# Expert layer: three-pass fp32r products, a fixed tile for each group and three more by index

## The chip, the core and the metric

The kernel runs on one core of a Trainium2 chip. The metric is device time in microseconds. Engines: TensorE (PE, its weight loads PEld), VectorE (DVE), ScalarE (ACT), GpSimd (POOL) and SyncE (SP, which here only issues DMAs).

## The reference

A block with two attention branches and a layer of hierarchical experts, then a second block. What the change touches is the expert layer on 512 rows `h` of width 1024:

```
g_sel  = argmax(h @ w_router_group + b)          # one of 8 groups for each row
top2   = top 2 of the 4 experts of that group    # by h @ w_router_expert
for e in 32 experts:
    hid = silu(h @ w_gate[e]) * (h @ w_up[e])    # 1024 -> 256
    out += (hid @ w_down[e]) * combine[:, e]     # 256 -> 1024, weight 0 if not chosen
```

`h` is the RMS norm of the residual `X` times the weights `norm_ffn_g`. All is float32.

## The kernel before

Rows are sorted by group, so that a tile of 128 rows needs only the four experts of its group. Block one (L949 to L1057) makes the norm (`Norm`, L277: squares on ScalarE, scaling of rows on VectorE into `XN`, transposes on TensorE, copies to `HT` with the norm weights as a scale for each partition), the router logits, the routing arithmetic on VectorE (some 60 small instructions), a slot number for each row (`SL_`) and for each unit the row numbers of its weights (`IX`). A group takes as many tiles of 128 as its count needs; eleven tiles (`NT`) are enough for any input. GpSimd then scatters the rows of `XN` with their four expert weights to `HS` in HBM. During this block SP loads three weight tiles for the block after the experts (L952).

Block two (L1089 to L1208) runs over 44 units n = 4j + x, tile j, expert x:

- GpSimd gathers the unit's weights by index: 2 MB into one of three `UP` (gate and up side by side, 8 x 512 columns), 1 MB into one of four `DN`.
- SP loads the tile's rows `HR` and stores the finished tile `OT` to `OS`.
- TensorE, step by step: the up product of unit n (8 f32 matmuls of 512 columns into `bank[n % 2]`), two transposes of the hidden rows of unit n-1, the down product of unit n-2 (4 f32 matmuls, summed over the tile's four units in two banks), and in steps 2 and 3 of a tile four transposes each of the next tile (`pe_tile`, L1072).
- ScalarE: silu of unit n (L1168), copy of the transposed hidden rows of n-1 (L1174), half of the output copy (L1181).
- VectorE: silu times up times the row's expert weight (L1194), half of the output copy (L1202), and at the end of a step the copy of the transposed tile times the norm weights into `HX` (`dve_tile`, L1082).

After the last unit GpSimd gathers the rows of `OS` back by slot and VectorE adds them to `X` (L1208). Every engine works through its list in order; waits are on counting semaphores, so an instruction also holds all that stands behind it on its engine. Each `nc.Block()` ends with all engines meeting. `sb2` gives a buffer a second name on the same memory for its fp32r content.

In other stages the kernel already multiplies split operands: ScalarE copies an operand rounded to fp32r (high part), VectorE subtracts that from the operand (low part), and TensorE makes three passes, low x high, high x low, high x high (L843 to L845, L2275 to L2277).

Of the kernel before, what the change touches and what calls it, by code (L numbers as in the profile page):

```python
# [83 lines left out]
def lay(i):  # L84
# [54 lines left out]
    for name, key in (("qd", "g_q_dil_2"), ("kd", "g_k_dil_2"), ("qm", "g_q_mem_2"), ("km", "g_k_mem_2")):  # L139
# [6 lines left out]
            "un": i["peer_u_2"][0], "vn": i["peer_v_2"][0], "grow": np.ascontiguousarray(np.broadcast_to(i["g_ffn_2"][0], (128, 1024))), "gains": g, "consts": consts, "bd": bd}, sizes  # L146
# [36 lines left out]
def program(nc, d, out, sizes):  # L183
    ctx = ExitStack()
    with ctx:
# [741 lines left out]
        NT = 11  # L927
        NU = 4 * NT
        HS, OS = d["hs"], d["os"]
        with ExitStack() as c0:  # L930
            XN = sb("XN", [128, 4, 1028], c0)
            SL_ = sb("slot", [128, 4], c0, I32)
            IX = sb("IX", [128, NU], c0, I32)
            scattered = sem("scattered", True)
            with ExitStack() as c1:
                norm = Norm(c1, "ffn", 1, 1, HT, "ffn", rows=XN)
                LG, GO, EX = sb("LG", [128, 4, 40], c1), sb("GO", [128, 4, 8], c1), sb("EX", [128, 4, 8], c1)
# [7 lines left out]
                GT, GI, IF = sb("GT", [128, NT, 8], c1), sb("GI", [128, NT], c1), sb("IF", [128, NT, 4], c1)  # L945
# [3 lines left out]
                with nc.Block() as block:  # L949
                    @block.sync  # L950
                    def _(e):
                        load_weights(e, 24)  # L952
# [18 lines left out]
                    @block.scalar  # L971
                    def _(e):
                        norm.act_sums(e)
                        norm.act_root(e)
                        norm.act_keep(e)
                        e.wait_ge(*e_off(1))
                        e.activation(EX, EX, ACT.Exp).then_inc(*e_exp.up(1))
                        e.wait_ge(*e_off2(1))
                        e.activation(s1[:, 3, :], s1[:, 2, :], ACT.Exp).then_inc(*e_exp2.up(1))

                    @block.vector
                    def _(e):
# [3 lines left out]
                        norm.dve_rows(e)  # L986
                        norm.dve_keep(e)
# [45 lines left out]
                        then(e.tensor_scalar(TL, RK[:, 4, :], 0.0, None, ALU.is_gt))  # L1033
                        for j in range(1, 4):
# [4 lines left out]
                        then(e.tensor_scalar(T9, T8, 128.0, None, ALU.mult))  # L1039
                        then(e.tensor_tensor(RK[:, 0:4, :], RK[:, 0:4, :], T9.unsqueeze(1).to_broadcast([128, 4, 8]), ALU.add))  # L1040
# [3 lines left out]

                        then(e.tensor_tensor(GT, EN.unsqueeze(1).to_broadcast([128, NT, 8]),
                                             col(cc("iota")[:, 0:NT]).to_broadcast([128, NT, 8]), ALU.is_le))
                        then(e.tensor_reduce(GI, GT, AX.X, ALU.add))
                        then(e.tensor_scalar(GI, GI, 7.0, 512.0, ALU.min, ALU.mult))
                        then(e.tensor_tensor(IF, cc("rows").unsqueeze(1).to_broadcast([128, NT, 4]), col(GI).to_broadcast([128, NT, 4]), ALU.add))
# [9 lines left out]
            UP = [sb(f"UP{n}", [128, 4096], c0) for n in range(2)] + [HT.rearrange("p k n -> p (k n)")]  # L1059
            DN = [sb(f"DN{n}", [128, 2048], c0) for n in range(4)]  # L1060
            HR = [sb(f"HR{n}", [128, 1028], c0) for n in range(2)]
            HX = [sb(f"HX{n}", [128, 8, 128], c0) for n in range(2)]
            SLU, HN = ([sb(f"{x}{n}", [128, 256], c0) for n in range(2)] for x in ("SLU", "HN"))
            HH = [sb(f"HH{n}", [128, 256], c0) for n in range(3)]
            OT = [sb(f"OT{n}", [128, 1024], c0) for n in range(2)]
            (m_hturn, m_hx, m_up, m_silu, m_hn, m_turn, m_hh, m_down, m_outA, m_outV, m_add) = sems(
                "m_hturn m_hx m_up m_silu m_hn m_turn m_hh m_down m_outA m_outV m_add")
            up_in, dn_in = [sem(f"up_in{n}", True) for n in range(3)], [sem(f"dn_in{n}", True) for n in range(4)]
            hr_in, os_done = [sem(f"hr_in{n}") for n in range(2)], [sem(f"os_done{n}") for n in range(2)]
            yg_in = sems("yg_in0 yg_in1 yg_in2 yg_in3", True)  # L1070

            def pe_tile(e, j, part):  # L1072

                if part == 0:
                    e.wait_ge(*hr_in[j % 2](16 * (j // 2) + 16))
                if 2 * j + part:
                    e.wait_ge(*m_hx(2 * j + part))
                for q in range(4):
                    i = e.transpose(bank[3][:, span(q)], HR[j % 2][:, span(4 * part + q)], ident)
                i.then_inc(*m_hturn.up(1))  # L1080

            def dve_tile(e, j, part):  # L1082
                e.wait_ge(*m_hturn(2 * j + part + 1))
                if j >= 2:
                    e.wait_ge(*m_up(4 * (j - 2) + 4))
                g4 = gg("ffn")[:, span(part, 4)].unsqueeze(2).to_broadcast([128, 4, 128])
                e.tensor_tensor(HX[j % 2][:, span(part, 4), :], bank[3].rearrange("p (a b) -> p a b", a=4), g4, ALU.mult).then_inc(*m_hx.up(1))  # L1087

            with nc.Block() as block:  # L1089
                @block.gpsimd  # L1090
                def _(e):
                    for n in range(NU):
                        off = bass.IndirectOffsetOnAxis(ap=IX[:, n:n + 1], axis=0)
                        if n >= 3:
                            e.wait_ge(*m_up(n - 2))
                        e.indirect_dma_start(UP[n % 3], None, d["wup"][:, :], off).then_inc(*up_in[n % 3].up(16))
                        if n >= 4:
                            e.wait_ge(*m_down(n - 3))
                        off = bass.IndirectOffsetOnAxis(ap=IX[:, n:n + 1], axis=0)
                        e.indirect_dma_start(DN[n % 4], None, d["wdn"][:, :], off).then_inc(*dn_in[n % 4].up(16))  # L1100
                    for n in range(2):
                        e.wait_ge(*os_done[n](16 * ((NT + 1 - n) // 2)))
# [5 lines left out]
                def _(e):  # L1108
                    e.wait_ge(*scattered(64))
                    for j in range(NT + 2):  # L1110
                        if j < NT:
                            if j >= 2:
                                e.wait_ge(*m_hn(4 * (j - 2) + 4))
                            e.dma_start(HR[j % 2], HS[span(j), :]).then_inc(*hr_in[j % 2].up(16))
                        if j >= 2:
                            e.wait_ge(*m_outA(j - 1))
                            e.wait_ge(*m_outV(j - 1))
                            e.dma_start(OS[span(j - 2), :], OT[j % 2]).then_inc(*os_done[j % 2].up(16))

                @block.tensor  # L1120
                def _(e):
                    pe_tile(e, 0, 0)
                    pe_tile(e, 0, 1)
                    for step in range(NU + 2):
                        n = step
                        if n < NU:
                            j = n // 4
                            e.wait_ge(*m_hx(2 * j + 2))
                            e.wait_ge(*up_in[n % 3](16 * (n // 3) + 16))
                            if n >= 2:  # L1130
                                e.wait_ge(*m_hn(n - 1))
                            for k in range(8):
                                i = e.matmul(bank[n % 2], HX[j % 2][:, k, :], UP[n % 3][:, span(k, 512)], start=k == 0, stop=k == 7)  # L1133
                            i.then_inc(*m_up.up(1))
                        n = step - 1
                        if 0 <= n < NU:
                            e.wait_ge(*m_hn(n + 1))
                            if n:
                                e.wait_ge(*m_hh(n))
# [4 lines left out]
                        if 0 <= n < NU:  # L1144
                            j, x = divmod(n, 4)
                            e.wait_ge(*m_hh(n + 1))
                            e.wait_ge(*dn_in[n % 4](16 * (n // 4) + 16))
                            if x == 0 and j >= 2:
                                e.wait_ge(*m_outA(j - 1))
                                e.wait_ge(*m_outV(j - 1))  # L1150
                            for half_ in range(2):
                                for q in range(2):
                                    i = e.matmul(bank[4 + 2 * (j % 2) + half_], HH[n % 3][:, span(q)], DN[n % 4][:, span(2 * q + half_, 512)],  # L1153
                                                 start=x == 0 and q == 0, stop=x == 3 and q == 1, skip_group_check=True)
                            i.then_inc(*m_down.up(1))
                        j, x = divmod(step, 4)
                        if x >= 2 and j + 1 < NT:
                            pe_tile(e, j + 1, x - 2)

                @block.scalar  # L1160
                def _(e):
                    for step in range(NU + 2):
# [7 lines left out]
                        if 0 <= n < NU:  # L1170
# [3 lines left out]
                            e.activation(HH[n % 3], bank[2][:, 0:256], ACT.Copy).then_inc(*m_hh.up(1))  # L1174
                        n = step - 2
                        if 0 <= n < NU and n % 4 == 3:
                            j = n // 4
                            e.wait_ge(*m_down(n + 1))
                            if j >= 2:
                                e.wait_ge(*os_done[j % 2](16 * (j // 2)))  # L1180
                            e.activation(OT[j % 2][:, 512:1024], bank[5 + 2 * (j % 2)], ACT.Copy).then_inc(*m_outA.up(1))  # L1181

                @block.vector
                def _(e):
                    dve_tile(e, 0, 0)
# [1167 lines left out]
```

## Time and profile before

| | us |
|---|---|
| runs | 3452.49, 3452.99, 3468.13 |
| median | 3452.99 |
| profiled execution, first to last instruction | 3467.7 |
| of it the expert block, first row load to the next block's first instruction | 672.4 to 1183.6 |

The page gives for the whole span TensorE 88% busy, VectorE 50%, ScalarE 31%, GpSimd 14%, and a mean granted clock of 0.93. These are means over some fifteen stages; the expert stage is read by itself. A busy TensorE is not TensorE at its peak, and the duration of a matmul record is longer than the distance to the next one, since matmuls overlap; rates are taken from starts. An f32 matmul leaves two records, an fp32r pass one.

### The profile page before, as it was taken

The page shows a single profiled execution, that of the slowest core. Times are in us where ns is not written, and L with a number is a line of the kernel's source. Part 1 is how long each engine was busy: PE and PEld are TensorE (multiplying, and loading weights), DVE is VectorE, ACT ScalarE, POOL GpSimd, SP SyncE. Part 2 cuts the span into 40 slices and gives each one's busy share as a digit, 9 for nine tenths or more (in the row PEclk, how much of TensorE's full clock was granted, in tenths as well). Part 3 has the DMA queues.
Part 4 walks back from the last instruction along what each step waited for, and adds up shares of the span by engine and source line. Part 5 has one row for each costly group of instructions (what it writes and reads, how often), then busy time and mean ns, then how long its engine had stood idle before and what let it go on. Part 6 is the DMA issues. An engine that isn't in the chain of part 4 may idle for free. (4 is left out here: it accounts for less than half of the span.)

```text
span 3467.7 us, 33649 instructions
## 1 busy us (share of the span) xinstructions
PE 3066.9 (88%) x12681; PEld 2229.5 (64%) x12681; DVE 1723.3 (50%) x3505; ACT 1076.1 (31%) x1596; POOL 488.8 (14%) x357
## 2 busy tenths in 40 slices
PE   7887999699999598778979879698898986999998
PEld 3445666444444244564746568698898986888887
DVE  2255422200000205543442328787879797788886
ACT  2133421100000126674421222234434443333332
POOL 0000000111111000000000000003314143344442
PEclk9995999699999798889779989899999998999999
DMA  3110061488888210021002211357859688999996
GB/s 142 44 50 25 1 145 64 194 329 309 313 315 309 85 49 37 25 97 44 1 26 102 83 55 61 123 193 246 324 178 336 233 305 292 342 369 374 368 374 238
DMA packets 159776, 624.04 MB, mean 180 GB/s; under 512 B 12161, under 2 KB 84481, under 8 KB 128257
## 3 DMA queue, kind: packets, MB, share of 16 engines
q1 hardware_dynamic: 90496, 319.87, 26.1%
q0 software_dynamic: 50688, 276.85, 21.1%
q10 hardware_dynamic: 18432, 25.17, 2.0%
q8 instruction: 102, 1.67, 0.2%
q14 instruction: 58, 0.47, 0.0%
HBM read 555.76 MB, written 66.09 MB: 179 GB/s over the span
## 5 line engine op out<-in xcount | busy, mean ns | idle before, releaser
L1841 POOL DMA_INDIRECT RG<-in_un,EI x128 | 181.6, 1419 | 1400.0 <-DVE EI L2060 1105.3
L2275 PE MATMUL bank<-VH,GL 128*128 128x512 f32 x768 | 300.2, 391 | 29.9 <-DVE VR0r L2264 29.9
L2277 PE MATMUL bank<-VH,GH 128*128 128x512 f32 x768 | 299.7, 390 | 0.0
L1841 POOL DMA_INDIRECT RG<-in_vn,EI x128 | 216.5, 1691 | 446.7 <-DVE X L1855 429.9
L1133 PE MATMUL bank<-UP,HX 128*128 128x512 f32 x480 | 213.0, 597 | 9.4 <-DVE HX L1087 5.5
L1194 DVE SCALAR_TENSOR_TENSOR HN<-SLU,HR,bank 128x256 f32<-128x256 f32 x44 | 21.1, 481 | 344.2 <-ACT SLU L1168 344.2
L2275 PEld LDWEIGHTS bank<-VH,GL 128*128 128x128 f32 x768 | 144.8, 189 | 60.7 <-issue 30.4
L1855 DVE SCALAR_TENSOR_TENSOR X<-RG,DG,X 128x1024 f32<-128x1024 f32 x128 | 164.1, 1282 | 28.2 <-DMA RG<-in_vn,EI 24.1
L1825 PE MATMUL bank<-HTl,UH1r 128*128 128x384 f32 x512 | 174.5, 341 | 0.0
L1826 PE MATMUL bank<-HTh,UH1r 128*128 128x384 f32 x512 | 174.2, 340 | 0.0
L1825 PE MATMUL bank<-HTl,UH0r 128*128 128x384 f32 x512 | 173.3, 338 | 0.0
L1826 PE MATMUL bank<-HTh,UH0r 128*128 128x384 f32 x512 | 173.0, 338 | 0.0
L618 PE MATMUL bank<-W,HT 128*128 128x512 f32 (+2 forms) x384 | 155.1, 558 | 19.1 <-ACT SU L685 14.4
L1445 PE MATMUL bank<-W,HT 128*128 128x384 f32 (+2 forms) x448 | 163.2, 523 | 8.3 <-ACT SV L1491 8.3
L1133 PEld LDWEIGHTS bank<-UP,HX 128*128 128x128 f32 x480 | 90.6, 191 | 119.9 <-issue 112.7
L1852 DVE CUSTOM_DVE_ANT_0 RG<-RG,HR 128x1024 f32<-128x1024 f32 x128 | 155.7, 1220 | 20.7 <-DMA RG<-in_un,EI 20.7
L2277 PEld LDWEIGHTS bank<-VH,GH 128*128 128x128 f32 x768 | 144.9, 189 | 30.3
L2259 ACT ACTIVATE VH<-VR 128x2048 fp32r<-128x2048 f32 x64 | 119.6, 1910 | 130.8 <-DMA VR<-in_vn 122.8
L1153 PE MATMUL bank<-DN,HH 128*128 128x512 f32 x352 | 158.2, 592 | 0.0
L2181 ACT ACTIVATE GA<-bank 128x384 f32<-128x384 f32 x128 | 62.8, 491 | 296.3 <-PE bank L1826 296.2
L2276 PE MATMUL bank<-VR0r,GH 128*128 128x512 f32 x384 | 150.5, 392 | 0.0
L2103 PE MATMUL bank<-OB,OA 128*128 128x128 f32 x768 | 107.5, 287 | 48.2 <-DVE OB L2095 48.2
(518 smaller groups left out, 6569.3 us busy)
## 6 DMA issues: line engine op xcount, KB each, us to landing
UR<-in_u SPq DMA_DIRECT2D x64, 1024.0 KB, 5.5
VR<-in_vn SPq DMA_DIRECT2D x32, 2048.0 KB, 9.2
W<-in_weights SPq DMA_DIRECT2D x20, 1536.0 KB, 7.3
W<-in_weights SPq DMA_DIRECT2D x14, 2048.0 KB, 8.2
aspill<-GA ACTq DMA_DIRECT2D x128, 192.0 KB, 2.0
wspill<-VR SPq DMA_DIRECT2D x12, 2048.0 KB, 9.2
WW<-wspill SPq DMA_DIRECT2D x32, 768.0 KB, 13.9
AV<-aspill SPq DMA_DIRECT2D x32, 768.0 KB, 16.0
```

The lines of the kernel that those rows point to most:

```text
L618: i = e.matmul(bank[n % 2][:, 0:nw], lhs(k, tb), w[:, span(k, nw)], start=k == 0, stop=k == KK[t] - 1)
L1133: i = e.matmul(bank[n % 2], HX[j % 2][:, k, :], UP[n % 3][:, span(k, 512)], start=k == 0, stop=k == 7)
L1153: i = e.matmul(bank[4 + 2 * (j % 2) + half_], HH[n % 3][:, span(q)], DN[n % 4][:, span(2 * q + half_, 512)], start=x == 0 and q == 0, stop ...
L1445: i = e.matmul(bank[4 + u % 2][:, 0:w], lhs(k), weight(t)[:, span(k, w)], start=k == 0, stop=k == 7)
L1825: e.matmul(bk, r(hi[:, k, :]), r(HL_[:, k, 0:NT3]), start=False, stop=False)
L1826: i = e.matmul(bk, r(hi[:, k, :]), r(HH_[:, k, 0:NT3]), start=False, stop=k == 7)
L1841: e.indirect_dma_start(RG[q % RR], None, d["un" if what == "u" else "vn"][:, :], off).then_inc(*row_in[q % RR].up(16))
L1852: e.tensor_tensor_reduce(RG[q % RR], RG[q % RR], HR3, 1.0, 0.0, ALU.mult, ALU.add, DT[:, s:s + 1]).then_inc(*r_used.up(1))
L1855: e.scalar_tensor_tensor(X[:, 3, :], RG[q % RR], DG[:, s:s + 1], X[:, 3, :], ALU.mult, ALU.add).then_inc(*r_used.up(1))
L2275: e.matmul(bk, r(gl[:, a, t]), r(vh[:, a, :]), start=g == 0 and a == 0, stop=False)
L2276: e.matmul(bk, r(gh[:, a, t]), r(vl[:, a, :]), start=False, stop=False)
L2277: i = e.matmul(bk, r(gh[:, a, t]), r(vh[:, a, :]), start=False, stop=g == 31 and a == 3)
```

## The change

- Tiles: each of the eight groups has one fixed tile, whose weights SP loads by plain DMAs (`load_up`, `load_dn`) without an index. Rows beyond 128 of a group go to three more tiles (`NO`), whose weights are gathered by index; an index beyond the table moves nothing. `SEQ` mixes the 32 fixed and 12 indexed units, one indexed after every 2.5. 44 units remain.
- Products: both are made in three fp32r passes. ScalarE rounds and VectorE subtracts the unit's weights (4096 and 2048 columns), the tile's transposed rows and the transposed hidden rows. High parts of weights lie in the memory of the three `W` buffers.
- Norm weights: `FR` holds them as rows; VectorE applies them with the row scale in one operation, so neither the copies to `HT` nor those of the tile need them.
- Routing block: SP loads `FR`, up weights of units 0 and 1 and down weights of units 0 to 2. The three weight tiles for the next block are loaded after the last output store.
- Output: one `OT` in place of two, copied by ScalarE alone; one pair of banks for fixed tiles and one for indexed.

```diff
-        NT = 11
-        NU = 4 * NT
+        NT, NO = 8, 3
+        NU = 4 * (NT + NO)
+        SEQ = []
+        for k in range(4 * NT):
+            SEQ.append((k // 4, k % 4))
+            for o in range(4 * NO):
+                if int(2.5 * (o + 1)) == k:
+                    SEQ.append((NT + o // 4, o % 4))
...
+        BUILDS = sorted(((FIRST_AT[t] - 2 + part, t, part) for t in range(NT + NO) for part in range(2)))
...
                     def _(e):
-                        load_weights(e, 24)
+                        e.dma_start(FR, d["frow"]).then_inc(*fr_in.up(16))
+                        load_weights(e, 21)
+                        load_up(e, 0)
+                        load_dn(e, 0)
+                        load_up(e, 1)
+                        load_dn(e, 1)
+                        load_dn(e, 2)
...
-                        norm.dve_rows(e)
-                        norm.dve_keep(e)
+                        norm.dve_scale(e)
+                        e.wait_ge(*fr_in(16))
+                        for b in range(4):
+                            e.scalar_tensor_tensor(XN[:, b, 0:1024], X[:, b, :], norm.o[:, b:b + 1], FR, ALU.mult, ALU.mult).then_inc(*n_rows.up(1))
...
+            def act_build(e, t, part):
+                b = BUILT[t, part]
+                e.wait_ge(*m_hturn(b + 1))
+                if before(t) >= 0:
+                    e.wait_ge(*m_up(LAST_AT[before(t)] + 1))
+                e.activation(r(HXh[place(t) - 1][:, span(part, 4), :]), bank[3].rearrange("p (a b) -> p a b", a=4), ACT.Copy).then_inc(*m_hxh.up(1))
+
+            def dve_build(e, t, part):
+                b = BUILT[t, part]
+                e.wait_ge(*m_hxh(b + 1))
+                s = span(part, 4)
+                e.tensor_tensor(r(HXl[place(t) - 1][:, s, :]), bank[3].rearrange("p (a b) -> p a b", a=4), HXh[place(t) - 1][:, s, :], ALU.subtract).then_inc(*m_hxl.up(1))
...
+            def act_up(e, n):
+                e.wait_ge(*(up_in if NORMAL(n) else up_over)[n % 3](nth(n)))
+                if n >= 2:
+                    e.wait_ge(*m_up(n - 1))
+                for half_ in range(2):
+                    c = span(half_, 2048)
+                    e.activation(r(UH[n % 2][:, c]), UP[n % 3][0][:, c], ACT.Copy).then_inc(*m_uph.up(1))
...
                 @block.sync
                 def _(e):
                     e.wait_ge(*scattered(64))
+                    for t in (0, 1, NT):
+                        load_rows(e, t)
+                    load_up(e, 2)
+                    for step in range(NU + 2):
+                        n = step + 3
+                        if n < NU and NORMAL(n):
+                            e.wait_ge(*m_up(n - 2))
+                            load_up(e, n)
...
+                        n = step + 1
+                        if 3 <= n < NU and NORMAL(n):
+                            e.wait_ge(*m_down(n - 2))
+                            load_dn(e, n)
+                        n = step - 2
+                        if 0 <= n < NU and SEQ[n][1] == 3:
+                            t = SEQ[n][0]
+                            e.wait_ge(*m_out(2 * ENDED.index(t) + 2))
+                            e.dma_start(OS[span(t), :], OT).then_inc(*os_done.up(16))
+                    load_weights(e, 24)
...
                 @block.tensor
...
+                            e.wait_ge(*m_hxl(BUILT[t, 1] + 1))
                             if n >= 2:
                                 e.wait_ge(*m_hn(n - 1))
                             for k in range(8):
-                                i = e.matmul(bank[n % 2], HX[j % 2][:, k, :], UP[n % 3][:, span(k, 512)], start=k == 0, stop=k == 7)
+                                if k % 4 == 0:
+                                    e.wait_ge(*m_upl(2 * n + k // 4 + 1))
+                                c = span(k, 512)
+                                e.matmul(bank[n % 2], r(xl[:, k, :]), r(wh[:, c]), start=k == 0, stop=False)
+                                e.matmul(bank[n % 2], r(xh[:, k, :]), r(wl[:, c]), start=False, stop=False)
+                                i = e.matmul(bank[n % 2], r(xh[:, k, :]), r(wh[:, c]), start=False, stop=k == 7)
...
+                        for t, part in builds(step):
+                            pe_build(e, t, part)
...
                 @block.scalar
...
                             if n >= 3:
                                 e.wait_ge(*m_down(n - 2))
-                            e.activation(HH[n % 3], bank[2][:, 0:256], ACT.Copy).then_inc(*m_hh.up(1))
+                            e.activation(r(HHh[n % 3]), bank[2][:, 0:256], ACT.Copy).then_inc(*m_hhh.up(1))
+                            act_down(e, n)
+                        n = step + 2
+                        if n < NU:
+                            act_up(e, n)
...
+                            if ENDED.index(t):
+                                e.wait_ge(*os_done(16 * ENDED.index(t)))
+                            for half_ in range(2):
+                                e.activation(OT[:, span(half_, 512)], bank[(4 if t < NT else 6) + half_], ACT.Copy).then_inc(*m_out.up(1))
+                        for t, part in builds(step):
+                            act_build(e, t, part)
...
                 @block.vector
...
+                        n = step - 1
+                        if 0 <= n < NU:
+                            e.wait_ge(*m_hhh(n + 1))
+                            e.tensor_tensor(r(HHl[n % 3]), bank[2][:, 0:256], HHh[n % 3], ALU.subtract).then_inc(*m_hhl.up(1))
+                            dve_down(e, n)
+                        n = step + 2
+                        if n < NU:
+                            dve_up(e, n)
+                        for t, part in builds(step):
+                            dve_build(e, t, part)
```

`dve_up`, `act_down` and `dve_down` follow the form of `act_up`: the subtraction waits for the rounding (of the same half), the low part is written over the loaded weights. Down weights are split in one piece of 2048 columns. `FIRST_AT[t]` is the place of a tile's first unit in `SEQ`.

## Rows read from the trace of the kernel before

**Rows 1.** Busy time by stretch: length, PE, PEld, DVE, ACT, POOL, PEclk, DMA share, GB/s

```profile
1000.00:1100.00 100.00, 98.43 (x254) 44.77 (x253) 9.16 (x16) 7.71 (x21) 16.86 (x18) 1.00 0.81 309
```

**Rows 2.** Timeline of TensorE: start, us, engine, line, operation, idle before and releaser

```profile
895.91 0.60 PE L1079 MATMUL bank<-C,HR 128*128 128x128 f32 x4
...
897.29 7.13 PE L1133 MATMUL bank<-HT,HX 128*128 128x512 f32 x16 [0.78 <-DVE HX L1087]
...
904.26 0.38 PE L1141 MATMUL bank<-C,HN 128*128 128x128 f32 x2
904.48 3.60 PE L1153 MATMUL bank<-DN,HH 128*128 128x512 f32 x8
907.92 7.03 PE L1133 MATMUL bank<-UP,HX 128*128 128x512 f32 x16
...
914.78 0.38 PE L1141 MATMUL bank<-C,HN 128*128 128x128 f32 x2
```

**Rows 3.** Timeline of TensorE in two stages with three fp32r passes

```profile
599.87 0.40 PE L843 MATMUL bank<-WH,YL 128*128 128x512 f32 x1
...
604.77 0.40 PE L843 MATMUL bank<-WH,YL 128*128 128x512 f32 x1
...
3300.15 0.39 PE L2275 MATMUL bank<-VH,GL 128*128 128x512 f32 x1
...
3302.19 0.39 PE L2275 MATMUL bank<-VH,GL 128*128 128x512 f32 x1
```

**Rows 4.** Timeline of ScalarE and VectorE, then two lines' durations (min/median/max)

```profile
904.46 0.38 ACT L1168 ACTIVATE SLU<-bank 128x256 f32<-128x256 f32 x1 [11.35 <-PE bank L1133]
...
2977.09 3.73 ACT L2259 ACTIVATE VH<-VR 128x2048 fp32r<-128x2048 f32 x2 [4.72 <-DMA VR<-in_vn]
...
629.58 2.74 DVE L302 TENSOR_SCALAR XN<-X,rtffn 128x1024 f32<-128x1024 f32 x4
...
1190.44 4.87 DVE L1290 SCALAR_TENSOR_TENSOR X<-X,rtfin,G 128x1024 f32<-128x1024 f32 x4
...
L2264 DVE TENSOR_TENSOR VR0r<-VR,VH x32: 2281/2286/2294, 2930.0 to 3429.9; 128x2048 fp32r<-128x2048 f32 x32
...
L1087 DVE TENSOR_TENSOR HX<-bank,G x22: 691/692/693, 676.9 to 1116.6; 128x512 f32<-128x512 f32 x22
```

**Rows 5.** Timeline of TensorE: restart and first pass at full rate, twice

```profile
580.21 0.80 PE L843 MATMUL bank<-WH,YL 128*128 128x512 f32 x1 [2.77 <-DVE YL L897]
...
583.30 0.39 PE L844 MATMUL bank<-W0r,YH 128*128 128x512 f32 x1
...
1993.80 0.80 PE L843 MATMUL bank<-WH,YL 128*128 128x512 f32 x1 [12.04 <-DVE YL L897]
...
2000.09 0.39 PE L843 MATMUL bank<-WH,YL 128*128 128x512 f32 x1
```

**Rows 6.** DMA issues: count, KB each, median us from issue to landing

```profile
W<-in_weights SPq DMA_DIRECT2D x14, 2048.0 KB, 8.2
...
UP<-in_wup,IX POOLq DMA_INDIRECT x30, 10.4
...
XN<-os,slot POOLq DMA_INDIRECT x4, 5.3
...
RG<-in_un,EI POOLq DMA_INDIRECT x128, 8.5
```

**Rows 7.** Timeline of SP's queue and TensorE around the expert stage

```profile
672.42 0.80 SPq L1114 DMA_DIRECT2D HR<-hs  x2
...
682.65 15.44 PE L1133 MATMUL bank<-UP,HX 128*128 128x512 f32 x32 [3.91 <-DMA UP<-in_wup,IX]
...
1155.88 0.38 PE L1141 MATMUL bank<-C,HN 128*128 128x128 f32 x2
```

**Rows 8.** Timeline of GpSimd and ScalarE at the stage's end

```profile
1170.44 0.94 POOL L1105 DMA_INDIRECT XN<-os,slot  x1 [30.58 <-DMA os<-OT]
...
1183.62 1.06 ACT L289 ACTIVATE xnfin<-X 128x1024 f32<-128x1024 f32 x1 [16.20 <-PEq L1089]
```

More of the change, by code:

```diff
@@ L974, in _ @@
                         norm.act_root(e)
-                        norm.act_keep(e)
+                        for k in range(0, 8, 2):
+                            e.wait_ge(*n_turn(8 + k + 1))
+                            e.activation(HT[:, k, :], bank[k], ACT.Copy).then_inc(*n_keptA.up(1))
                         e.wait_ge(*e_off(1))
@@ L1032, in _ @@
                         then(e.tensor_copy(RK, bank[1][:, 0:40].rearrange("p (b g) -> p b g", b=5)))
-                        then(e.tensor_scalar(TL, RK[:, 4, :], 0.0, None, ALU.is_gt))
-                        for j in range(1, 4):
+                        then(e.tensor_scalar(TL, RK[:, 4, :], 128.0, None, ALU.is_gt))
+                        for j in range(2, 4):
                             then(e.tensor_scalar(T8, RK[:, 4, :], 128.0 * j, None, ALU.is_gt))
@@ L1064, in program @@
[L1064 to L1069, printed above, removed]
@@ L1070, in program @@
-            yg_in = sems("yg_in0 yg_in1 yg_in2 yg_in3", True)
-            def pe_tile(e, j, part):
+            UH = [W2[0][1], W2[1][1]]
+            DH = [W2[2][1][:, span(n, 2048)] for n in range(2)]
+            OT = XN[:, 0, 0:1024]
+            place = lambda t: 1 + (t % 2 if t < NT else 2)
+            HR = lambda t: XN[:, place(t), :]
+            HXh, HXl = ([sb(f"{x}{n}", [128, 8, 128], c0) for n in range(3)] for x in ("HXh", "HXl"))
+            SLU, HN = ([sb(f"{x}{n}", [128, 256], c0) for n in range(2)] for x in ("SLU", "HN"))
@@ new lines, in program @@
+            HHh, HHl = ([sb(f"{x}{n}", [128, 256], c0) for n in range(3)] for x in ("HHh", "HHl"))
+            (m_hturn, m_hxh, m_hxl, m_uph, m_upl, m_dnh, m_dnl, m_up, m_silu, m_hn, m_turn, m_hhh, m_hhl, m_down, m_out, m_add) = sems(
+                "m_hturn m_hxh m_hxl m_uph m_upl m_dnh m_dnl m_up m_silu m_hn m_turn m_hhh m_hhl m_down m_out m_add")
+            hr_in, os_done = [sem(f"hr_in{n}") for n in range(3)], sem("os_done")
+            yg_in = sems("yg_in0 yg_in1 yg_in2 yg_in3", True)
@@ L1089, in program, with dve_down @@
+            def dve_down(e, n):
+                e.wait_ge(*m_dnh(n + 1))
+                e.tensor_tensor(r(DN[n % 3][1]), DN[n % 3][0], DH[n % 2], ALU.subtract).then_inc(*m_dnl.up(1))
             with nc.Block() as block:
@@ L1091, in _ @@
                 def _(e):
[L1092 to L1102, printed above, removed]
+                    for step in range(-3, NU):
+                        n = step + 3
+                        if 2 <= n < NU and not NORMAL(n):
+                            x = 4 * (SEQ[n][0] - NT) + SEQ[n][1]
+                            if n >= 3:
+                                e.wait_ge(*m_up(n - 2))
+                            e.indirect_dma_start(UP[n % 3][0], None, d["wup"][:, :], bass.IndirectOffsetOnAxis(ap=IX[:, x:x + 1], axis=0),
+                                                 bounds_check=4095, oob_is_err=False).then_inc(*up_over[n % 3].up(16))
+                        n = step + 1
+                        if 3 <= n < NU and not NORMAL(n):
+                            x = 4 * (SEQ[n][0] - NT) + SEQ[n][1]
+                            e.wait_ge(*m_down(n - 2))
+                            e.indirect_dma_start(DN[n % 3][0], None, d["wdn"][:, :], bass.IndirectOffsetOnAxis(ap=IX[:, x:x + 1], axis=0),
+                                                 bounds_check=4095, oob_is_err=False).then_inc(*dn_over[n % 3].up(16))
+                    e.wait_ge(*os_done(16 * (NT + NO)))
                     for tb in range(4):
```

167 lines of the change are left out of this document (99 added, 68 removed).

## Prediction

> **What bounds the kernel now.** The changed stage is the expert stage: 44 units (11 tiles of 128 token rows, 4 experts each). [...] The timeline of TensorE says what it does in a unit: two transposes (0.22 us), 8 records of the down product (3.44 us), 16 records of the up product (6.86 us), together 10.52 us from one unit to the next, with nothing idle [rows 2]. A full f32 matmul is two records of 0.43 us, 0.86 us. Each tile also takes two groups of four transposes (0.44 us each at 0.11 us, the spacing of the unit's two), and after the second TensorE waits for VectorE's copy: 1.38 us in all, of which 0.94 is this wait [rows 2]. Remember that wait: the second group sits directly ahead of the tile's first up product, and the change lengthens what lies between.
>
> **What the change removes and adds on TensorE.** Each product of a split f32 pair is three fp32r passes. The trace has such triples in two other stages: seven triples in 4.90 us (0.233 us a pass) and three in 2.04 us (0.227) [rows 3]. I take 0.230 and keep both ends. Three passes are 0.69 us against 0.86. A unit becomes 24 passes up (5.52), 12 down (2.76) and the transposes (0.22): 8.50 us against 10.52. If that were all, 44 units would save some 85 us. The number of units stays 44: the three tiles by index are computed whether filled or not. [...]
>
> **What it adds on ScalarE and VectorE.** For each unit ScalarE now rounds 4096 + 2048 columns of weights to fp32r and VectorE subtracts them. The price is that of the last stage's split: a ScalarE copy of 2048 columns, two in 3.73 us, so 1.82 us apiece with a 1.91 us end-to-end; a VectorE subtraction 2.29 us, and 2.20 from start to start, since consecutive VectorE instructions overlap by about 0.08 (four of 1.28 us take 4.87) [rows 4]. ScalarE: 0.38 + 0.38 + 3 x 1.82, plus copies for tiles, about 6.5 to 8 us a unit. VectorE: 0.48 + 0.4 + 3 x 2.20, about 7.5, plus 0.69 in steps with a tile build. Both are under 8.50, so neither sets the steady pace. That is not the end of it, since the order within the queues matters.
>
> **The new wait.** Call U the moment when TensorE has issued the up product of unit s. ScalarE then does silu, the copy of the hidden rows and the down rounding (ends U + 2.7: 0.2 from the transposes at 904.26 to silu at 904.46 [rows 2, 4], 0.28 for each of the two small ones, 1.91), then the two up roundings for unit s+2, ending U + 4.5 and U + 6.3. VectorE waits for the down rounding, and does its three subtractions from U + 2.7: ends at U + 5.0, 7.2, 9.4. Only then, last in its step, stands the subtraction for the tile being built (0.69 us, as the same shape in [rows 4]), ending at U + 10.0. The second half of a tile is built in the step just ahead of the tile's first unit, so the next up product waits for that: it can start at U + 10.15, whereas TensorE has finished transposes, down product and build at U + 0.22 + 2.76 + 0.44 = U + 3.4. TensorE idles 6.7 us. In steps with no second half the up product needs only what VectorE did a step earlier (slack over 4 us), and the down product likewise. The order of units puts second halves in steps 2, 4, 10, 15, 16, 21, 26, 30, 32 and 38: ten stalls. The ScalarE copy of the tile (about 0.6) and the output copies come before it, but end by U + 7.8 and are hidden under VectorE; if VectorE were idle they would cost at most 2 us.
>
> **The clock after each stall.** [...] Half rate for 4.5 us loses 4.5 x (1 - 0.230/0.427) = 2.1 us; bounds 1.4 and 2.9. So a step with a stall is 10.15 + 5.52 + 2.1 = 17.8 us, against 8.50 without and 8.94 with a first half.
>
> **Loads.** The 32 fixed units are loaded by SP with plain DMAs, 2 MB up and 1 MB down. SP issues the up load of unit n when the up product of n-3 is done, and ScalarE wants it 10.8 us later or more (11.5 ahead of a stall). A plain 2 MB load lands in 8.2 us [rows 6], so it is hidden, by 2.6 us; late loads would show in the stalls one for one. On SP, the row loads and the output stores stand behind waits that end by U + 7.8, before the next load is due. The reference's router, worked out on the given inputs, sends 52 to 75 tokens to each of the 8 groups, so no group exceeds 128 and the three indexed tiles are empty: their 12 units have indexes beyond the table. No row shows what a gather costs whose rows all are out of bounds; it lies between nothing and a full load (10.4 us as now [rows 6]), and both ends are hidden under the 10.8 us. What it does bring is less traffic, which nothing waits for.
>
> **Before the loop.** The norm weights on the rows: four three-operand row operations cost 4.87 us where four scalings cost 2.74 [rows 4], and the transposes follow them: +2.1. The scale-free copies out of PSUM save under 0.1 and I take zero. The slot arithmetic has one small VectorE instruction more, 0.2. So all engines enter the expert block 2.3 us later, at 674.7 instead of 672.4 [rows 7]. The 7 MB loaded early have landed by then, so the wait for the first weights (3.91 us [rows 7]) goes, but what is late next is VectorE: it splits unit 0 first (to 681.1), then the first half of tile 0 (681.7), TensorE turns the second half at half clock (1.1, twice the 0.60 of [rows 2] less overlap), ScalarE copies 0.6, VectorE subtracts 0.7: first up product at 684.3, against 682.65. If ScalarE's table load stands first instead of ahead of the first silu, 1.3 more.
>
> **The sum.** U(0) = 684.3 + 5.5 + 2.1 = 691.9. U(1) = 697.4. U(2) = 703.1. In step 2 VectorE is still 3.5 us behind from the start, so the third up product starts at 715.6, and U(3) = 723.2. From there 40 steps: 9 stalls x 17.8, 0.4 for the double build in step 15, 31 x 8.50, 8 first halves x 0.44: 427.6. U(43) = 1150.8, against 1155.88 now [rows 7]. The 2.0 us a unit bring some 85 us, ten stalls take 67, the clock takes 23 with the one at the start, and the old stage's own waits (10 x 0.94) are gone: what is left is 5.
>
> **The end.** Now the final gather starts 14.6 us after U(43) [rows 7, 8]. After: the down split of unit 42 holds its product till U + 5.1, that of unit 43 till U + 8.0, and its output copy must wait for the store of the indexed tile from the same single buffer (about 2.8 us from store to release): gather at U + 16.2, +1.6. The gather of the outputs then competes with three 2 MB weight loads that formerly ran during routing and now are issued right behind the last store. Gathers of this size land in 5.3 us there now, and in 8.5 us in the stage with saturated DMA [rows 6]: I take +3.6 for the last of four, bounds 0 and 7. The weights themselves are needed 26 us after the next block's start and land in time. Sum: 1150.8 + 16.2 + 13.2 (gather to next block [rows 8]) + 3.6 = 1183.8, against 1183.62: **no change**. The profiled execution took 3467.7 us; the runs were 3452.49, 3452.99 and 3468.13, so the profile resembles the highest. No difference against the median gives 3453. Terms of the range: pass interval +-5 (1464 passes on the path by 0.0033), clock -7 to +10, gather +-3.5, start +1.3, length of stalls +-3: roughly 3440 to 3465 for this case by itself.
>
> **Rivals.**
> Clock kept (faster): were the clock not lowered by the ten 6.7 us stalls, 21 us would come back: 3432. Against: every row with more than 2.7 us idle shows it lowered.
> [...]
> No stall (faster): if VectorE reached the tile's subtraction before U + 3.4, stalls and clock losses vanish: about -88 us, 3365. It needs VectorE to reorder or to be three times as quick; its subtraction times vary under 1%.
> [...]
> Late weights (slower): if plain loads land later than 11.5 us after issue, every stall grows by the excess. The output stores, row loads and down loads share the queue; the same size lands in 8.2 us at the median but the gathers now in 10.4. At 13.8 us: 10 x 2.3, 3476.
> That the change doesn't do what it says: the three passes and the queue order stand in the code, so there is little room; included in the above.
>
> **How the numbers follow.** Forecast 0.68, clock kept 0.07, pace of the clock 0.03, no stall 0.04, half clock long 0.08, late weights 0.10. Within 0.5% (17 us, about what a measurement of this kernel can tell from no change) lies the forecast but for 0.04 on either side. Faster: 0.14 + 0.04 = 0.18. Slower: 0.18 + 0.04 = 0.22. Same: 0.60. The range goes from just below the kept clock (3430) to just past the late weights (3478).
>
> **What would show it.** Right: a spacing of 8.5 us between up products, ten gaps of 6 to 7 us on TensorE each released by VectorE's tile subtraction, passes of 0.43 us behind each, a mean clock in the stage near 0.9, U(43) near 1151. Wrong: gaps released by a DMA or by ScalarE's rounding (late weights), passes at full rate behind gaps, a steady spacing above 9 us (then VectorE or ScalarE sets the pace).

## The result

| | median, us | ratio of the fast runs to those of before | 95% interval |
|---|---|---|---|
| before | 3452.99 | 1 | |
| after | 3471.26 | 1.0035 | 1.002 to 1.005 |

The change made the kernel slower by 0.35% (0.2 to 0.5%), some 12 us. The forecast was no change (3453, within 17 us). The profiled execution of after has a span of 3491.4 us against 3467.7, but 16.1 of these 23.7 us arise ahead of the changed stage, in an attention stage that the change doesn't touch (last section). So the profiles are compared by stage, each from its own start: from the first instruction of the routing block to the first of the block behind the experts it was 560.9 us (622.76 to 1183.62) and is 569.0 (638.87 to 1207.87), 8.1 us more.

The page of after, shares of the span:

```profile
PE 3021.3 (87%) x13209; PEld 2351.6 (67%) x13209; DVE 2022.8 (58%) x3672; ACT 1329.7 (38%) x1761; POOL 435.7 (12%) x293
...
UP<-in_wup SPq DMA_DIRECT2D x22, 2048.0 KB, 8.0
DN<-in_wdn SPq DMA_DIRECT2D x32, 1024.0 KB, 7.3
```

VectorE and ScalarE have 300 and 254 us more work, TensorE 46 less, and yet the span isn't shorter. The busy time by stretch in the middle of the expert stage (length, PE, PEld, DVE, ACT, POOL, granted clock, DMA share, GB/s) answers to [rows 1]:

```profile
755.00:1100.00 345.00, 299.49 (x1262) 239.38 (x1263) 239.49 (x170) 203.03 (x187) 25.45 (x18) 0.91 0.59 224
```

TensorE was 98% busy at clock 1.00 and set the pace of the stage; now it is 87% busy at 0.91. It waits, and it is slowed. Where, the timeline around tile 9 shows. TensorE (answers to [rows 2]):

```profile
877.34 0.38 PE L1256 MATMUL bank<-C,HN 128*128 128x128 f32 x2
877.47 0.48 PE L1271 MATMUL bank<-W2r,HHl 128*128 128x512 f32 x1
...
880.34 0.60 PE L1138 MATMUL bank<-C,XN 128*128 128x128 f32 x4
887.38 0.79 PE L1246 MATMUL bank<-W1r,HXl 128*128 128x512 f32 x1 [6.44 <-DVE HXl L1152]
...
888.82 0.63 PE L1246 MATMUL bank<-W1r,HXl 128*128 128x512 f32 x1
890.10 0.63 PE L1246 MATMUL bank<-W1r,HXl 128*128 128x512 f32 x1
...
893.73 0.39 PE L1246 MATMUL bank<-W1r,HXl 128*128 128x512 f32 x1
894.43 0.39 PE L1246 MATMUL bank<-W1r,HXl 128*128 128x512 f32 x1
895.13 0.39 PE L1246 MATMUL bank<-W1r,HXl 128*128 128x512 f32 x1
895.83 0.38 PE L1256 MATMUL bank<-C,HN 128*128 128x128 f32 x2
```

ScalarE and VectorE in the same step:

```profile
877.53 0.38 ACT L1290 ACTIVATE SLU<-bank 128x256 f32<-128x256 f32 x1 [6.00 <-PE bank L1248]
877.81 0.38 ACT L1296 ACTIVATE HHh<-bank 128x256 fp32r<-128x256 f32 x1
878.08 1.92 ACT L1175 ACTIVATE W2r<-DN 128x2048 fp32r<-128x2048 f32 x1
879.88 3.71 ACT L1163 ACTIVATE W0r<-UP 128x2048 fp32r<-128x2048 f32 x2
...
877.95 0.48 DVE L1325 SCALAR_TENSOR_TENSOR HN<-SLU,XN,bank 128x256 f32<-128x256 f32 x1 [5.70 <-ACT SLU L1290]
...
880.03 2.29 DVE L1179 TENSOR_TENSOR DN0r<-DN,W2r 128x2048 fp32r<-128x2048 f32 x1 [1.26 <-ACT W2r L1175]
882.24 4.48 DVE L1169 TENSOR_TENSOR UP0r<-UP,W0r 128x2048 fp32r<-128x2048 f32 x2
886.64 0.68 DVE L1152 TENSOR_TENSOR HXl<-bank,HXh 128x512 fp32r<-128x512 f32 x1
```

TensorE has turned the second half of the tile by 880.9. VectorE subtracts down weights, then both halves of the up weights, and the 0.68 us that TensorE waits for come last. They begin at 886.64, although ScalarE's copy that they need was made by 885.04 (0.61 us from 884.43, L1146): the engine takes its list in order. The pause is 6.44 us, and the three-pass rounds behind it start 1.28 us apart (0.43 a pass), against 0.70 us from 893.73 on. There are ten such pauses: nine of 6.4 to 6.5 us and a first one of 7.3. Elsewhere the spacing of units is 8.60 to 8.62 us, and 9.0 in a step with a first half.

The sum of the stage in us, in parts that begin and end at the same instructions:

| part | before | after | forecast for after |
|---|---|---|---|
| routing block, to the first row load | 49.7 | 48.6 | 52.0 |
| first row load to first up product | 10.2 | 9.7 | 9.6 |
| first up product to the transposes behind the last one | 473.2 | 472.6 | 466.5 |
| from there to the first output gather | 14.6 | 16.3 | 16.2 |
| that to the next block | 13.2 | 21.9 | 16.8 |

### The profile page after: what moved, and what is told of

Read it like the earlier page. It is cut to its first block and busy times, and to the rows that moved or that the text cites. A ratio compares the mean times of both kernels' runs of the same rounds, so it can differ in the third digit from the quotient of the medians.

```text
span 3491.4 us, 35116 instructions
## 1 busy us (share of the span) xinstructions
PE 3021.3 (87%) x13209; PEld 2351.6 (67%) x13209; DVE 2022.8 (58%) x3672; ACT 1329.7 (38%) x1761; POOL 435.7 (12%) x293
## 3 DMA queue, kind: packets, MB, share of 16 engines
q0 software_dynamic: 41472, 138.45, 10.8%
## 5 line engine op out<-in xcount | busy, mean ns | idle before, releaser
L1955 PE MATMUL bank<-HTh,UR0r 128*128 128x384 f32 x352 | 122.4, 348 | 31.3 <-DVE UR0r L1944 31.3
L2407 PE MATMUL bank<-VR1r,GH 128*128 128x512 f32 x384 | 149.4, 389 | 0.0
L1576 PEld LDWEIGHTS bank<-W,HT 128*128 128x128 f32 x448 | 97.0, 232 | 75.1 <-issue 47.8
L619 PEld LDWEIGHTS bank<-W,HT 128*128 128x128 f32 x384 | 71.3, 190 | 94.3 <-issue 75.8
```

Of the source, the lines that this page charges most:

```text
L619: i = e.matmul(bank[n % 2][:, 0:nw], lhs(k, tb), w[:, span(k, nw)], start=k == 0, stop=k == KK[t] - 1)
L1576: i = e.matmul(bank[4 + u % 2][:, 0:w], lhs(k), weight(t)[:, span(k, w)], start=k == 0, stop=k == 7)
L1955: e.matmul(bk, r(lo[:, k, :]), r(HH_[:, k, 0:NT3]), start=k == 0, stop=False)
L2407: e.matmul(bk, r(gh[:, a, t]), r(vl[:, a, :]), start=False, stop=False)
```

## Experiments

Each is an edit to the changed kernel. Beside the ratio, "loop" is the time from the start of the first tile's second-half transposes to the start of the last transposes of hidden rows. It starts 2.5 us ahead of the first up product (5.0 in before and 1.9 in "f32"), though two of the expectations call its start the first up product, and ends a unit further than in the table: before 481.9, after 478.1 us. From the first up product it is 476.9 and 475.6.

**The weight loads behind the gathers.**

```diff
+                    for tb in range(4):
+                        e.wait_ge(*yg_in[tb](16))
                     load_weights(e, 24)
```

> One edit to the changed kernel: SP issues the three 2 MB weight loads for the next block only after the four gathers of the expert output have landed. Theory (the gathers share the DMA engines with these loads): from the first gather to the next block's first instruction 13 us, as in the kernel before, instead of 21.9 us; total 8 to 9 us less than the changed kernel, ratio to the kernel before about 1.001; the loads now end some 17 us later and are still in time, since the next block wants them 26 us after its start. Rival (the gathers themselves got slower, by their place or by the waits ahead of them): still about 22 us, total as the changed kernel, ratio 1.0035. Second rival: the weights come too late for the next block, and a wait for W of several us stands ahead of its first product; total unchanged.

Measured: ratio 0.9986 (0.9956 to 1.0015), loop 476.5. From gather to next block 11.3 us, 10.6 less than after. Times to landing of the four gathers, and the next block's first instruction (after first, then this kernel):

```profile
XN<-os,slot POOLq DMA_INDIRECT x4, 16.2
1185.93 0.95 POOL L1201 DMA_INDIRECT XN<-os,slot  x1 [27.67 <-DMA os<-XN]
1207.87 1.06 ACT L290 ACTIVATE xnfin<-X 128x1024 f32<-128x1024 f32 x1 [25.15 <-PEq L1181]
```

```profile
XN<-os,slot POOLq DMA_INDIRECT x4, 5.5
1160.82 0.96 POOL L1201 DMA_INDIRECT XN<-os,slot  x1 [27.36 <-DMA os<-XN]
1172.14 1.06 ACT L290 ACTIVATE xnfin<-X 128x1024 f32<-128x1024 f32 x1 [14.21 <-PEq L1181]
```

The gathers took three times as long beside the loads, and without them as long as in [rows 6]. The theory holds. Both rivals fall: no wait for weights appears ahead of the next block's first product. The loads cost the gathers more than the comparison with before shows: 10.6 us here, where after was only 8.8 above before. The rest lies behind the last addition to `X`, which the next block followed by 2.8 us in before and by 0.3 and 0.6 in the two kernels here; why is open. The ratio alone, with its interval, would not settle 9 us; the trace does.

**Filling the pause.**

```diff
-                            e.wait_ge(*m_hxl(BUILT[t, 1] + 1))
                             if n >= 2:
                                 e.wait_ge(*m_hn(n - 1))
+                            if n in FIRST_AT.values() and n not in (0, 16):
+                                for _ in range(7):
+                                    e.matmul(bank[n % 2], ident, C[:, 0:512], start=True, stop=True)
+                            e.wait_ge(*m_hxl(BUILT[t, 1] + 1))
```

> One edit to the changed kernel: ahead of the first up product of a tile (9 of the 10 stalls, not the one in step 15) TensorE makes 7 f32 matmuls of constants into the bank that the up product will overwrite; their result is used by nothing. They fill about 6.0 of the 6.4 us in which TensorE was idle. Clock theory: no pass of 0.43 us is left behind these stalls, a step with a stall falls from 18.1 to 15.8 us, total 9 x 2.3 = 21 us less than the changed kernel, ratio to the kernel before about 0.997; granted clock in the stage 0.99 instead of 0.91. Rival (the slow passes come with the new tile, not with the idle time): still 18.1 us and ratio 1.0035 or, where the filling outlasts the stall, more.

Measured: ratio 0.9956 (0.9919 to 0.9993), loop 458.0, 20.0 us less than after. Not one slow pass is left behind the nine filled pauses; 11 stand behind the one that was left alone. One filled pause, and the busy time by stretch:

```profile
718.77 6.17 PE L1243 MATMUL bank<-C 128*128 128x512 f32 x14
...
740.00:1060.00 320.00, 310.99 (x1308) 235.77 (x1307) 236.56 (x169) 202.50 (x185) 25.42 (x18) 0.98 0.64 238
```

TensorE does work of no use, waits just as long for VectorE, and the loop is 20 us shorter: the clock term, by itself. The nine filled steps took 143.4 us in place of 164.6, 2.35 us less each; the one left alone took 1.2 us more.

**The tile ahead of the up weights.**

```diff
                             dve_down(e, n)
+                        for t, part in builds(step):
+                            dve_build(e, t, part)
                         n = step + 2
                         if n < NU:
                             dve_up(e, n)
-                        for t, part in builds(step):
-                            dve_build(e, t, part)
```

(and the same on ScalarE)

> One edit to the changed kernel: within a step ScalarE copies and VectorE subtracts the tile being built before the weights of unit s+2 instead of after them. Theory (the stall is VectorE's two weight subtractions that stand ahead of the tile's): the tile is ready at U + 5.8 instead of U + 10.1, so the idle time falls from 6.4 to about 2 us; with an idle time that short the clock may stay: 10 x 4.4 = 44 us less if the clock falls as before, 67 us less if it stays; ratio 0.991 or 0.984. Rival (ScalarE's rounding or the loads hold the tile): the stall moves by less than 1 us and the ratio stays above 1.001.

Measured: ratio 0.985 (0.980 to 0.991), loop 417.3, 60.8 us less. One step:

```profile
765.58 2.29 DVE L1179 TENSOR_TENSOR DN0r<-DN,W2r 128x2048 fp32r<-128x2048 f32 x1 [0.44 <-ACT W2r L1175]
767.79 0.68 DVE L1152 TENSOR_TENSOR HXl<-bank,HXh 128x512 fp32r<-128x512 f32 x1
768.98 4.49 DVE L1169 TENSOR_TENSOR UP0r<-UP,W0r 128x2048 fp32r<-128x2048 f32 x2 [0.51 <-ACT W0r L1163]
...
768.53 0.51 PE L1246 MATMUL bank<-W1r,HXl 128*128 128x512 f32 x1 [2.02 <-DVE HXl L1152]
```

The pause follows the place of one instruction in VectorE's list: 2.02 us in place of 6.43. The two weight subtractions were the pause, as the theory says; ScalarE and the loads were not. The first pause fell from 7.27 to 3.70 us. 10 x 4.4 gives 44 us. The rest is clock: of 107 slow passes (records longer than 0.6 us) 28 are left, and 79 x (0.427 - 0.233) = 15 us. The result lies between the two figures expected, because after 2.0 us of pause the clock fell in some cases (four stretches) and not in others.

**The tiles one step earlier.**

```diff
-BUILDS = sorted(((FIRST_AT[t] - 2 + part, t, part)
...
+BUILDS = sorted(((FIRST_AT[t] - (2 if t in (0, NT + 1, NT + 2) else 3) + part, t, part)
...
```

> One edit to the changed kernel: the tiles 1 to 8 are built one step earlier (the two last indexed tiles as they were, since their rows share one buffer). Theory: eight of the ten stalls vanish with their slow passes, 8 x 9.1 = 73 us and 1.5 more for the longer one in step 2; two stalls remain, at tiles 9 and 10; total about 3397 us, ratio 0.982 (0.0035 above 1 less 0.0215). Rival (VectorE becomes the bound once TensorE no longer waits, since it needs 8.3 us a unit in steps with a build): spacing of up products above 9 us over whole tiles, and a ratio above 0.987.

Measured: ratio 0.981 (0.976 to 0.987), loop 407.7, 70.4 us less than after (expected 74). Two pauses of 6.43 us remain, the second followed by one of 1.41, with 20 slow passes. VectorE does not become the bound: it has 1.0 to 1.2 us idle in a step, ahead of the down subtraction:

```profile
881.63 2.29 DVE L1179 TENSOR_TENSOR DN2r<-DN,W2r 128x2048 fp32r<-128x2048 f32 x1 [1.03 <-ACT W2r L1175]
883.84 4.49 DVE L1169 TENSOR_TENSOR HTr<-HT,W1r 128x2048 fp32r<-128x2048 f32 x2
888.25 0.47 DVE L1325 SCALAR_TENSOR_TENSOR HN<-SLU,XN,bank 128x256 f32<-128x256 f32 x1
...
890.25 2.29 DVE L1179 TENSOR_TENSOR DN0r<-DN,W2r 128x2048 fp32r<-128x2048 f32 x1 [1.20 <-ACT W2r L1175]
```

**The change without the split.** f32 products in both places, with no rounding and no subtraction; TensorE waits for the loads themselves. Of the edit, the up product:

```diff
-                                e.matmul(bank[n % 2], r(xl[:, k, :]), r(wh[:, c]), start=k == 0, stop=False)
-                                e.matmul(bank[n % 2], r(xh[:, k, :]), r(wl[:, c]), start=False, stop=False)
-                                i = e.matmul(bank[n % 2], r(xh[:, k, :]), r(wh[:, c]), start=False, stop=k == 7)
+                                i = e.matmul(bank[n % 2], xh[:, k, :], UP[n % 3][0][:, span(k, 512)], start=k == 0, stop=k == 7)
```

> The changed kernel with plain f32 products: nothing is rounded or subtracted, the up and down products read the loaded weights as f32; fixed tiles, indexed tiles, direct loads, row norm weights, single output buffer and late weight loads stay. It prices the rest of the change without the split. Theory: units of 10.5 us as in the kernel before, TensorE waits about 0.9 us at each tile; loop within 3 us of the 481.9 us of before; start 2 to 3 us shorter (no weight split first), gather to next block 21.9 us as in the changed kernel: total +6 us, ratio 1.002, so that the split as built brings nothing (changed kernel 1.0035). Rival (the direct loads by themselves make the stage faster, and the split eats it): loop below 470 us and a ratio under 0.999.

Measured: ratio 1.0009 (0.9981 to 1.0038), loop 479.1; gather to next block 21.9. Units are 10.52 us apart and the wait at a tile is short (0.7 us, 1.2 in two places):

```profile
896.63 7.13 PE L1244 MATMUL bank<-HT,HXh 128*128 128x512 f32 x16 [1.23 <-ACT HXh L1146]
903.61 0.38 PE L1252 MATMUL bank<-C,HN 128*128 128x128 f32 x2
...
914.12 0.38 PE L1252 MATMUL bank<-C,HN 128*128 128x128 f32 x2
```

Loop 479.1 without the split, 478.1 with it; from the first up product 477.3 and 475.6. That is the whole gain of three passes as they were put in: 1 to 2 us, and for the whole stage there is none left, 567.2 us without the split and 569.0 with it. The two ratios don't tell them apart, since their intervals overlap. Fixed tiles and direct loads bring nothing in the loop either (476.9 us before from the first up product), since the loads were hidden before (no up product but the first waited for a DMA); they only take away the wait for the first weights, 3.9 us.

**Without the indexed tiles** (the computation of the three indexed tiles is left out; on these inputs no row belongs to them).

```diff
-        NU = 4 * (NT + NO)
+        NU = 4 * NT
...
-                if int(2.5 * (o + 1)) == k:
+                if False:
...
```

> The changed kernel without the 12 units of the three indexed tiles (their computation is left out; on these inputs no row belongs to them; three finished tiles are stored twice so that all of the output table is written). It tells what these units cost and how near the loads are. Theory: 12 x 8.6 us and the three stalls of these tiles, 3 x 9.5, go: loop 478 - 132 = 346 us, ratio to the kernel before about 0.965. Rival (the indexed units gave the queue the time to catch up; 32 units with 3 MB each in 8.6 us leave no slack): waits for UP or DN appear ahead of ScalarE's rounding, the spacing of up products exceeds 8.9 us, and the ratio stays above 0.97.

Measured: ratio 0.963 (0.959 to 0.967), loop 343.0, 135.1 us less than after (expected 132). The busy time by stretch:

```profile
740.00:1000.00 260.00, 221.40 (x938) 176.84 (x937) 181.69 (x130) 153.04 (x141) 0.00 (x0) 0.92 0.80 313
```

ScalarE shows no wait for a load in this stretch, though the DMA share is 0.80; the loads aren't the bound even here. The twelve indexed units cost TensorE as much as real ones; what they save is only traffic. By the DMA packets recorded, an index beyond the table moves nothing: the queue of the gathers (q0 of the page) carried 276.85 MB in before, 138.45 in after and 138.44 here, where 24 gathers fewer are made. Their times in after:

```profile
UP<-in_wup,IX POOLq DMA_INDIRECT x8, 2.2
HT<-in_wup,IX POOLq DMA_INDIRECT x4, 3.0
DN<-in_wdn,IX POOLq DMA_INDIRECT x12, 4.4
```

(issue to landing in after, where all indexes are out of bounds; the up gathers against 10.4 us in [rows 6]).

**Three edits together**: the earlier tiles, the tile ahead of the weights, the loads behind the gathers.

> The changed kernel with three edits together: tiles 1 to 8 built one step earlier, the tile ahead of the weights in each step of ScalarE and VectorE, and the three weight loads behind the output gathers. From the single runs: the loop as with the earlier builds (407.7 us from the first up product to the last transposes) less two stalls that shrink from 6.4 to 2.0 us and lose their slow passes, 2 x 6.7, gives 394 us; end as with the late weights, 11.3 us from gather to next block instead of 21.9. Together 84 + 10.6 = 95 us less than the changed kernel: ratio to the kernel before about 0.976. Rival (with no idle time left VectorE or the loads set the pace): a spacing of up products above 8.7 us over whole tiles and a ratio above 0.983.

Measured: ratio 0.972 (0.969 to 0.976), median 3370.99 us; this beats both kernels. Loop 396.1, gather to next block 11.3:

```profile
740.00:1060.00 320.00, 314.53 (x1402) 252.97 (x1401) 272.28 (x192) 229.78 (x208) 29.10 (x19) 0.98 0.70 265
...
1091.92 1.06 ACT L290 ACTIVATE xnfin<-X 128x1024 f32<-128x1024 f32 x1 [14.21 <-PEq L1181]
```

TensorE is 98% busy again. The changed stage is 89.8 us shorter than in after and 81.7 shorter than before, which would be a ratio of 0.976. Another 14 us or so of the measured difference lie outside it; see the last section.

## Why the prediction came out as it did

The median fell 18 us above the forecast of 3453, and by the ratio the true effect is 12 us. That is inside the range (3430 to 3478). The forecast case by itself gave 3440 to 3465: the median lies 6 us above that, and 3453 plus the 12 us of the ratio lies at its upper end. The mechanism was right, and a few terms were too small. Part of the agreement is luck: the stage was forecast within 0.2 us of before and came out 8.1 longer, the sum of 6.1 too little for the loop, 5.1 too little for the end and 3.4 too much for the routing block, which mostly a higher granted clock made shorter (2.5 us in the logits). Without those 3.4 us the stage would have been 11 us longer.

- **The new wait** stood where it was put: up product at U + 10.04 (877.34 to 887.38) against U + 10.15, steps 2, 4, 10, 15, 16, 21, 26, 30, 32 and 38, released by VectorE's tile subtraction (in step 15 it holds the next tile's transposes). Moving the instruction moved the pause ("order"), an earlier build removed it ("early").
- **The clock after each pause**: 2.35 us, by the nine steps of "fill", against 2.1. The slow time from restart was taken as 4.5 us, the mean of seven restarts by fp32r passes in the trace of before (slow for 3.1 to 6.3 us, 0.427 us a pass, after idle times of 2.77 to 30.8 us); ahead of the nine up products it was 4.0 to 6.1, 5.2 on average, and 5.2 x (1 - 0.233/0.427) is 2.4.
- **Steady unit**: 8.61 against 8.50. The pass took 0.233 us, the upper of the two spacings in [rows 3], where the step took 0.230. Over 31 plain steps that is 3.4 us. A step with a pause took 18.10 us on average (nine of them) against 17.8, with the 0.4 of step 15 2.3 us more in all. With 0.4 in the first steps they are the 6 us by which the loop was undersized.
- **Loads hidden**: right. In the loop ScalarE waits for no load. A plain 2 MB load lands in 8.0 us at the median, and gathers that are all out of bounds in 2.1 to 6.3 us.
- **Before the loop**: engines enter a block together (SP's first row load and ScalarE's first instruction at 672.42 and 672.44 us in before, 687.44 and 687.47 in after). The block entry was to come 2.3 us later and came 1.1 earlier in the profile of after, where the logits ran at a higher granted clock (64 small matmuls in 9.6 us at 0.74, against 12.1 at 0.58 before). In "late_w" they took 12.0 again, at 0.58, and the block 51.7 us, 2.0 more than before (2.3 forecast). So the added VectorE work costs about what was said. Of the nine profiles, three show the logits at 12.0 to 12.2 us (before, "late_w" and the three edits together) and six at 9.6 to 9.9; what decides it is open.

```profile
L999 PE MATMUL bank<-W,HT 128*128 128x40 f32 x64 | 9.6, 329 | 0.8 <-ACT HT L1015 0.8
```

- **The gather beside the weight loads**: the term that failed. Taken as +3.6 with bounds 0 and 7; it was +8.8, and by "late_w" 10.6. The step read the price of contention off a stage where gathers of 0.5 MB alternate with loads (8.5 us to landing). Here three loads of 2 MB stood queued when the gathers came, and those took 16.2 us. No run varied how many loads were queued, so the depth is the likely cause, not a shown one. The nearest row had the right kind but not the right depth of queue.
- **Start and single output buffer**: 9.7 against 9.6 and 16.3 against 16.2. The four transposes of a second half took 1.11 us there. ScalarE's table load (1.28 us) began at 699.93, behind the start of the first up product (697.09), so its 1.3 us did not come in.

The rivals: "clock kept", "no stall", "late weights" and "half clock long" did not occur. The last needed 24 passes of 0.427 us, 10.2 us, behind a pause (the slow stretches were of 4.0 to 6.1 us from the restart, counted as in [rows 5], and one of 3.0 in step 15). The ground given against "clock kept", that every idle time over 2.7 us lowers it, held for these ten pauses but not in "order", where one of 3.70 us did not (last section). "Pace of the clock", passes closer than the 0.227 us of [rows 3], did not occur either: they came 0.233 apart.

## What to carry to other kernels

When work is moved from the bounding engine to idle ones, busy shares don't say whether it is hidden: ask which instruction the bounding engine waits for, and count what now stands ahead of it in each in-order queue. Here 18% less TensorE time in a unit (8.61 us against 10.52) was given back by one small subtraction behind two large ones. Moving it made the changed kernel 1.8% faster, starting it a step earlier 2.2%, and both with the late loads 3.1%, which is 2.8% below before. And a pause on TensorE can be paid twice, here 6.4 us as idle time and 2.35 in clock. Here the loads for the next stage belong behind the transfers that end the present one: the four gathers took 16.2 us beside them and 5.5 ahead of them.

## What the runs showed of the hardware that was not expected

- The length of a pause alone doesn't decide whether the granted clock falls. In "order" slow passes stand behind four of nine pauses of 2.0 to 2.1 us, 7 each, in two cases from the restart and in two over 1 us later. Behind the longest pause of that loop, 3.70 us, there is none. The shortest with a fall in the trace of before was 2.77 us [rows 5]. The passes behind 3.70 us, and behind one of 2.01:

```profile
693.34 0.50 PE L1246 MATMUL bank<-W1r,HXl 128*128 128x512 f32 x1 [3.70 <-DVE HXl L1152]
693.68 0.39 PE L1247 MATMUL bank<-UP0r,HXh 128*128 128x512 f32 x1
...
875.85 0.80 PE L1246 MATMUL bank<-W0r,HXl 128*128 128x512 f32 x1 [2.01 <-DVE HXl L1152]
876.44 0.63 PE L1247 MATMUL bank<-UP1r,HXh 128*128 128x512 f32 x1
```

- A gather whose indexes are all out of bounds still costs time: for up weights 1.0 us on GpSimd and 2.1 to 4.1 us to complete, for down weights mostly 1.9 and 3.0 to 6.3 us.
- The unchanged attention stage varies. The busy time and the granted clock by stretch, in before, after and the kernel with three edits:

```profile
280.00:360.00 80.00, 71.94 (x248) 51.13 (x249) 32.93 (x123) 31.18 (x102) 0.00 (x0) 0.53 0.00 1
360.00:420.00 60.00, 59.55 (x393) 44.74 (x391) 27.84 (x70) 27.15 (x67) 0.00 (x0) 1.00 0.00 1
```

```profile
280.00:360.00 80.00, 72.01 (x236) 51.32 (x237) 30.80 (x117) 30.36 (x100) 0.00 (x0) 0.50 0.00 1
360.00:420.00 60.00, 60.00 (x279) 41.61 (x278) 24.36 (x64) 24.18 (x61) 0.00 (x0) 0.76 0.00 1
```

```profile
280.00:360.00 80.00, 71.09 (x322) 51.84 (x323) 39.01 (x139) 37.39 (x121) 0.00 (x0) 0.69 0.00 1
```

TensorE is as busy in all three, but it is granted the full clock for more or less of the time, and that moves the time by more than the change does: before and after are level at 343 us and 15.2 us apart at 372, with the same work done. Of the nine profiles five show 0.50 to 0.53 between 280 and 360 us and four 0.69 to 0.73. What decides it stays open; no run varied it alone. It also isn't settled why a pass takes 0.233 us here and 0.227 in the last stage, at the same granted clock.
